# Retention branch projection: eight sums over one half of the features, then the other, and two expert weights' places in SBUF

## What is computed

```python
y_a = o_gla.astype(u.dtype) @ w_br_gla                  # (256, 1024) @ (1024, 1024)
y_b = o_ret.astype(u.dtype) @ w_br_ret                  # (256, 2048) @ (2048, 1024)
merged = (jax.nn.sigmoid(mga.astype(jnp.float32)) * y_a.astype(jnp.float32)
          + jax.nn.sigmoid(mgb.astype(jnp.float32)) * y_b.astype(jnp.float32))
return merged.astype(u.dtype) @ w_out                   # (256, 1024) @ (1024, 1024)
...
def run_block(args):                                    # experts: all 32, 6 MB of weights each
    e, tok, w = args
    xb = t[tok]
    hid = jax.nn.silu(xb @ wg[e]) * (xb @ wu[e])
    return ((hid @ wd[e]).astype(jnp.float32) * w[:, None])
```

## Time and profile before

| | |
|---|---|
| median of 3 executions | 1547.41 us (1546.74, 1547.41, 1552.07) |
| the profiled execution's own time | 1544.61 us |
| its span in the trace | 1543.3 us |
| PE busy / DVE / ACT over the span | 91% / 56% / 44% |
| granted TensorE clock, mean | 0.972 |
| dense work of block 1, retention branch within it | 0 to 428 us, 357 to 403 us |
| router | 428 to 441 us |
| experts | 441 to 875 us |
| block 2 | 875 to 1543 us |

### The profile page before, as it was taken

How to read it: one execution, slowest core, us unless ns; L and a number is a source line. 1 busy time by engine, 2 the same in 40 slices (tenths; PEclk the granted TensorE clock), 3 DMA queues, 4 the chain that set the end, 5 groups by cost and what they waited for, 6 DMA issues and landing times.

```text
span 1543.3 us, 27434 instructions
## 1 busy us (share of the span) xinstructions
PE 1405.4 (91%) x11609; PEld 1190.4 (77%) x11609; DVE 865.6 (56%) x1558; ACT 682.1 (44%) x1185; POOL 10.6 (1%) x10
## 2 busy tenths in 40 slices
PE   7999999999989867777777699999999999899998
PEld 7999899899966434443443389999999986699997
DVE  6776463475522211211121378988888768688776
ACT  6544454553442111111111366565555467565553
POOL 1000000000000000000000010000000000000000
PEclk9999999999989998999999999999999999999999
DMA  7455354469799999999999744236555333446551
GB/s 239 145 159 162 110 167 135 164 209 336 285 409 424 426 425 422 426 426 425 425 426 426 299 157 140 95 114 209 194 184 190 127 124 104 142 153 203 191 180 66
DMA packets 170641, 372.05 MB, mean 241 GB/s; under 512 B 6912, under 2 KB 137088, under 8 KB 145936
## 3 DMA queue, kind: packets, MB, share of 16 engines
q1 hardware_dynamic: 170512, 370.22, 64.4%
HBM read 369.15 MB, written 1.05 MB: 240 GB/s over the span
## 4 chain that ended last, share of the span: by engine, by line
PE 63%; DMA 22%; DVE 8%; ACT 5%; issue 2%; SPq 1%; DVEq 0%; ACTq 0%
PE bank L602 16%; PE bank L604 16%; PE bank L603 16%; DMA wu<-in_expert_w_up_dram 16%; PE bank L1724 4%; DMA wu<-in_expert_w_down_dram 3%; DVE lo L566 3%; ACT hi L555 2%; PE bank L833 2%; PE bank L1696 2%; PE bank L1762 1%; PE bank L1776 1%; DMA raw<-in_w_in_dram 1%; PE bank L942 1%; PE bank L967 1%
## 5 line engine op out<-in xcount | busy, mean ns | idle before, releaser
L566 DVE TENSOR_TENSOR lo<-raw,hi 128x1024 fp32r<-128x1024 f32 (+2 forms) x315 | 376.4, 1217 | 176.7 <-ACT hi L555 175.9
L602 PE MATMUL bank<-XH,hi 128*128 128x256 f32 x1416 | 405.7, 286 | 5.8 <-DVE lo L566 2.7
L603 PE MATMUL bank<-XL,hi 128*128 128x256 f32 x1416 | 400.7, 283 | 0.0
L604 PE MATMUL bank<-XH,lo 128*128 128x256 f32 x1416 | 400.7, 283 | 0.0
L555 ACT ACTIVATE hi<-raw 128x1024 fp32r<-128x1024 f32 (+2 forms) x315 | 321.4, 1049 | 117.8 <-PE bank L604 70.8
L602 PEld LDWEIGHTS bank<-XH,hi 128*128 128x128 f32 x1416 | 271.4, 192 | 14.0 <-issue 10.6
L603 PEld LDWEIGHTS bank<-XL,hi 128*128 128x128 f32 x1416 | 271.4, 192 | 0.8
L604 PEld LDWEIGHTS bank<-XH,lo 128*128 128x128 f32 x1416 | 271.3, 192 | 0.0
L1724 PE MATMUL bank<-wu,xg 128*32 128x256 f32 x2048 | 168.5, 429 | 57.0 <-DMA wu<-in_expert_w_up_dram 51.6
L1724 PEld LDWEIGHTS bank<-wu,xg 128*32 128x32 f32 x2048 | 72.0, 120 | 129.2 <-DMA wu<-in_expert_w_up_dram 69.5
L1762 PE MATMUL bank<-wu,hidT 128*32 128x256 f32 x1024 | 73.8, 402 | 35.6 <-DMA wu<-in_expert_w_down_dram 25.1
(11 more groups left out here) (383 smaller groups left out, 2173.4 us busy)
## 6 DMA issues: line engine op xcount, KB each, us to landing
wu<-in_expert_w_gate_dram SPq DMA_DIRECT2D x64, 1024.0 KB, 26.7
wu<-in_expert_w_up_dram SPq DMA_DIRECT2D x64, 1024.0 KB, 26.5
wu<-in_expert_w_down_dram SPq DMA_DIRECT2D x64, 1024.0 KB, 26.8
raw<-in_w_in_dram SPq DMA_DIRECT2D x44, 1024.0 KB, 5.2
raw<-in_ffn_w_up_dram SPq DMA_DIRECT2D x44, 1024.0 KB, 5.0
raw<-in_ffn_w_down_dram SPq DMA_DIRECT2D x22, 1024.0 KB, 5.0
raw<-in_hgrn_w_in_dram SPq DMA_DIRECT2D x16, 1024.0 KB, 5.4
raw<-in_w_branch_ret_dram SPq DMA_DIRECT2D x8, 1024.0 KB, 6.7
```

The costliest lines, as they stand in the source:

```text
L566: dve.tensor_tensor(lo_of(u), v, hi_of(u), ALU.subtract).then_inc(*WL.inc(u))
L602: pe.matmul(dst, first[0], first[1], start=start, stop=False)
L603: pe.matmul(dst, second[0], second[1], start=False, stop=False)
L604: return pe.matmul(dst, third[0], third[1], start=False, stop=stop)
```

## The change

All eight sums are now open at once, in eight PSUM banks. PE goes through the first half of the features for sums 0 to 7 (units 97 to 104), then through the second half for sums 0 to 7 (units 105 to 112). The weight tiles are taken in that order. A sum is therefore finished at each of the last eight units, where before two were finished at the end of each four. `act_split` and `dve_split` run one unit further ahead of the steps of a sum: eight splits stand alone (for units 97 + i), and in the loop over the sums the split of unit 108 + i comes before the steps of sum i.

Places 8 and 9 of the expert weights are now two that are free once the first half of the features is done (`us_at + 8192 * 5` and `gla_at`, where the first half of `RH` and `RL` lie). Their loads wait for unit 104 in place of unit 112 and are issued after tile 55 in place of after tile 59. Load 10 now stands ahead of tile 60, in their old place.

```diff
-    for i in range(4):
-        for h in range(2):
+    for h in range(2):
+        for i in range(4):
             add(cols(D, w_re[D * h:D * h + D, :], 256 * i), halves_c)
...
-    where += [us_at + 8192 * i for i in (5, 6, 7)] + [gla_at, gla_at + 8192] + [us_at + 8192 * i for i in (0, 1)]
+    where += [us_at + 8192 * 5, gla_at] + [us_at + 8192 * i for i in (6, 7)] + [gla_at + 8192] + [us_at + 8192 * i for i in (0, 1)]
...
         def re_unit(t, i):
 
-            return 2 * (t - i % 2) + 1 + i % 2
+            return 2 * t + 7 + i
+
+        def re_bank(t, i):
+
+            return (t + i) % 4 if i < 4 else i
...
+            sp.wait_ge(*WU.got(2 * 52))
+            sp_weights(8)
+            sp_weights(9)
             while at_tile[0] < TILES1 - 1:
                 sp_tile()
             sp.wait_ge(*WU.got(2 * 56))
-            sp_weights(8)
-            sp_weights(9)
+            sp_weights(10)
             sp_tile()
-            for n in range(10, 13):
+            for n in (11, 12):
                 sp_weights(n)
...
-            for i in range(0, 8, 2):
-                bs = bank[t % 4], bank[(t + 1) % 4]
...
+            for h in range(2):
+                for i in range(8):
+                    b, u = bank[re_bank(t, i)], 2 * t - 1 + 8 * h + i
+                    for s, key in b.taken if h == 0 else []:
                         pe.wait_ge(*s.got(*key))
...
+                    b.taken = [(MIX.dve, ("re", i))]
+            t += 8
...
             for i in range(8):
-                act_split(re_unit(t, i) + 3)
+                act_split(2 * t - 1 + i + 4)
+            for i in range(8):
+                act_split(re_unit(t, i) + 4)
                 act.wait_ge(*MIX.dve.got("merged", i))
...
             for i in range(8):
-                dve_split(re_unit(t, i) + 3)
+                dve_split(2 * t - 1 + i + 4)
+            for i in range(8):
+                dve_split(re_unit(t, i) + 4)
                 dve.wait_ge(*WU.got(re_unit(t, i)))
                 dve.wait_ge(*MIX.act.got("mb", i // 2))
-                dve.tensor_tensor(sig_b[:, i, :], b_[t % 4][:, 0:T], sig_b[:, i, :], ALU.mult).then_inc(*MIX.dve.inc("re", i))
+                dve.tensor_tensor(sig_b[:, i, :], b_[re_bank(t, i)][:, 0:T], sig_b[:, i, :], ALU.mult).then_inc(*MIX.dve.inc("re", i))
```

More of the change, by code:

```diff
@@ L1330, in pe_mixer @@
                 t += 1
-            for i in range(0, 8, 2):
-                bs = bank[t % 4], bank[(t + 1) % 4]
-                for b in bs:
-                    for s, key in b.taken:
+            for h in range(2):
+                for i in range(8):
+                    b, u = bank[re_bank(t, i)], 2 * t - 1 + 8 * h + i
+                    for s, key in b.taken if h == 0 else []:
                         pe.wait_ge(*s.got(*key))
[L1336 to L1349, removed]
+                    pe.wait_ge(*WH.got(u))
+                    pe.wait_ge(*WL.got(u))
+                    for k in range(8):
+                        kk = 8 * h + k
+                        pe.wait_ge(*RET.act.got("RH", kk // 4))
+                        pe.wait_ge(*RET.dve.got("RL", kk // 4))
+                        done = three(b.ap[:, 0:T], hi_of(u)[:, k, :], lo_of(u)[:, k, :], RH[:, kk, :], RL[:, kk, :],
+                                     False, kk == 0, kk == 15)
+                    done.then_inc(*WU.inc(u))
+                    b.taken = [(MIX.dve, ("re", i))]
+            t += 8
             merged = lambda k: [(MIX.act, ("OH", k)), (MIX.dve, ("OL", k))]
@@ L1419, in act_mixer @@
                 act.activation(OH[:, i, :], sig_a[:, i, :], ACT.Copy).then_inc(*MIX.act.inc("OH", i))
-                t += 1
+            t += 8
             for i in range(4):
```

## The result

The changed kernel takes 1556.71 us (median of 17, 1548.72 to 1561.08), the kernel before 1546.91 (median of 17). The ratio is 1.0056, 95% interval 1.0045 to 1.0067: slower by 8.7 us (the medians alone differ by 9.8), a little over the 0.5% that was named as the bound. The forecast was 1552.2 us, slower by 4.8, with a range up to 1557.0, so the result lies only just inside it. The direction, the place and the mechanism came out; the size was nearly double. Two terms were too small: the clock, and what DMA loses behind load 22.

The account below looks back on a forecast made before the run. PE bounds the retention branch, DMA the experts. Stall 4.4 plus clock 1.7 make PE 6.1 us late; less 3.2 of queued work, plus 1.4 restart and 0.5 refill: +4.8, 1552.2 us, range 1545.5 to 1557.0.

Parts of the forecast that it names:

- Nothing to win on PE: Retention branch: PE is already busy throughout with the same 384 matmuls, so the new order of sums costs or wins 0.
- The bunched steps: Border to `o1`: eight rounds of 3.46 us exceed PE's 2.85 us unit, so PE resumes 4.4 us late.
- tile 56 would hold the ring: Sums' chain of waits: tile 56, queued behind loads 8 and 9, lands late and delays the rounds by 1.0 us.
- splits one unit ahead keep PE fed for free: Retention sums: low parts ready at least 1.4 us before PE needs them, 0.4 with the late tile; no cost.
- The clock, +1.7: `o1` after the stall: one stretch of 3.41 us at half clock costs half its length, 1.7 us.
- the refill, +0.5: Experts behind load 22: loads 24 and 25 wait on PE until the queue is deep again, 0.5 us.
- The sign that DMA would be full from load 22 on: Expert stream in the trace after: DMA at full rate from load 22, issued at about 450 us.
- The early loads: Loads 8 and 9: 4.9 us of transfer moved out buy nothing beyond 3.2 us; the queue runs dry before load 22.
- (A): Border to `o1`: same stall without low clock, PE 4.4 us late, total 1550.5 us; chance 0.25.
- (B): `o1` and router: three low stretches cost 5.1 us, router up to 1 more, stream 8.7 us late, 1556.1 us; chance 0.11.
- (C): Steps of the sums: rounds stay under 2.85 us, PE wins 0.4 us, stream 2.2 us earlier, 1545.2 us; chance 0.11.
- (D): Expert stream: both early loads count in full, 4.9 us, plus PE's 0.4, giving 1542.1 us; chance 0.03.

Follow-up runs that it names:

- the ring cut: Changed kernel with DVE's split of unit 108 + i moved behind the product and addition of sum i: 1544.11 us, ratio 0.9983.
- the second trace: Trace of the changed kernel measured once more, nothing altered: 1555.87 us, ratio 1.0048 to the kernel before.
- the last pair of kernels: Changed kernel with the DVE split moved later and 32 unread matmuls in the router's gap, loads 8 and 9 early or late: 0.9966 and 0.9979.
- Filling the stall: Changed kernel plus 27 unread matmuls on PE before its waits for sums 6 and 7 in `o1`: ratio 1.0019.
- the kernel before with the stall of 3.6 us: Kernel before, with DVE forming the router's weights eight times before `OL` of sum 7: ratio 1.0034.
- the fillings: Changed kernel with unread matmuls at the `o1` stall (27), in the router's gap (32), or both: ratios 1.0019, 1.0027, 1.0004.
- With the loads back: Changed kernel with loads 8 and 9 and their places returned to where they were, after tile 59: ratio 1.0049.
- ring cut, loads back: Changed kernel with the DVE split moved later and loads 8 and 9 back after tile 59: ratio 0.9986.
- A gap of 1.64 us: Kernel before, with DVE forming the router's weights four times before `OL` of sum 7: ratio 1.0004.

## Why the prediction came out as it did

**Nothing to win on PE: right.** The retention branch is full in both traces (46.30 of 46.30).

**The bunched steps: right, with one slip.** From the last gated step, unit 112 was to end at 45.6 and PE to go on at 52.8 (410.0 - 357.16). It went on at 53.2 (408.89 - 355.70). That is 4.8 us later than before (405.58 - 357.16 = 48.4) where 4.4 was forecast, a little above the bound. Rounds of 3.46 us were forecast and 3.45 to 3.56 measured where no tile was late, 3.95 and 4.22 where tiles 55 and 56 were. That tile 56 would hold the ring was right, tile 55 wasn't seen. The slip is the claim that splits one unit ahead keep PE fed for free: the first gap, 0.98 us, is PE waiting for the low part of unit 114 (`lo` ends at 403.53, PE goes on at 403.63). `o1` takes its second unit after four k-steps, not after eight, and the slack was counted as if each unit lasted 2.85 us. It cost nothing, since `OL` of sums 6 and 7 came later still; the ring cut shows this bunching and nothing else made the slowdown (0.9983).

**The clock, +1.7, and the refill, +0.5: these terms were too small.** Two stretches at half clock followed in place of one. They began inside the gap, at 406.80, where PE went on at 408.89: PE was busy for 4.74 of these 6.83 us, so `o1` itself lost 2.4 us (3.0 in the second trace, busy for 6.01). Load 22 came 7.3 and 7.6 us late where 6.1 was forecast. The larger miss lies behind it. There the sum took off 3.2 us for the work left in the queue and added 1.4 for the restart and 0.5 (bounds 0 and 1.8) for loads 24 and 25, -1.3 in all. DMA was 8.3 and 11.6 us behind, so the two traces have +1.0 and +4.0 at this step. Where the router's low stretch went on into the first experts, DMA starved a second time, since at half clock PE gives places back more slowly than DMA fills them; the two traces of the ring cut, 10.2 and 30.7 us of low clock with load 22 at the same point, show it: DMA is 7.3 us further behind in the second. Between them stand only the two loads, worth 1.5 us in the same measure in the last pair of kernels, and the stretch at 54 us, which the first has and the second has not. Filling the stall brought 4.5 to 5.7 us back in the total where 1.7 was forecast. The sign that DMA would be full from load 22 on failed too. In the changed kernel's trace the stretch from load 22 to 505 us runs below the rate of the earlier trace rows:

```profile
450.00:505.00 55.00, 54.30 (x714) 35.74 (x718) 13.02 (x32) 15.13 (x50) 0.00 (x0) 0.99 0.97 396
```

(396 GB/s, and 370 from 450 to 505 us in the second trace, against 413; a part of this is the restart of the dry queue.) In the kernel before with the stall of 3.6 us, whose router was slow for 30.7 us, it is plainer, here beside the kernel before:

```profile
456.00:468.00 12.00, 12.00 (x91) 6.97 (x94) 1.01 (x4) 3.52 (x10) 0.00 (x0) 0.50 0.48 181
```

```profile
456.00:468.00 12.00, 12.00 (x178) 8.16 (x174) 2.83 (x7) 3.85 (x14) 0.00 (x0) 1.00 1.01 412
```

181 GB/s over 12 us against 412 is 6.5 us of transfer missing (231 x 12 / 425), with PE busy all the time and doing half the matmuls. What settles how long the router stays slow is open: 30.7 us turn up with a stall and without one. Each kernel has one trace or two, and the totals scatter by 3.5 to 12 us within a kernel, so a trace alone doesn't tell whether a stall lengthens it. That the delay raises the mean of the total by more than its length is shown by the changed kernel (4.8 us late at `o1`, 7.0 to 10.4 in the total) and by the fillings, which leave the wait in place and take the total down to 1.0004.

The Trainium skill, in TensorE: Matmul & The Clock Gate, section on HAM oscillation, prices a kernel that waits between matmuls at half of its time at the low clock. By that, the 6.8 us cost 3.4. Here PE was idle for part of them and lost 2.4 to 3.0, and filling the gap was worth 4.5 to 5.7 in the total, likely because loads wait for PE's products.

**The early loads: right that they buy nothing here.** The queue ran dry between load 21 (landed at 436.81 + 9.9 = 446.7) and load 22, as drawn: 6 GB/s from 446 to 450 us. It was short of work earlier too, 154 GB/s from 428 to 432, since load 17 waits for a unit of the late `o1`. The signs had this dip (429 to 433), but the sum's 442.5 for the dry queue left it out. With the loads back the ratio is 1.0049, with them early 1.0048 and 1.0056: no gain and no loss that can be told.

**The rivals.** (A), the same stall at full clock, was put at 1550.5 us, 3.1 over; the kernel that realises it (stall filled) is 0.0019 or 2.9 us over (interval 1.1 to 4.6). PE went on 5.2 us late there and not 4.4, so the terms without the clock at `o1` are near in sum, which does not say that each is right. (B) came nearest to the result in size, 8.7 us for 8.7, and its sign, a second low stretch in `o1`, was there. But it had one stretch more at `o1` than there was, too little at the router, and left out the 0.5 for the refill; that the two numbers are equal is luck. It had a chance of 0.11; with gaps of 2 to 4 us followed by anything from none to three such stretches in the earlier trace rows, that chance was too low. (C) and (D) needed what the ring cut shows: once the round is below PE's unit, the change does win, 2.6 us (C had 2.2 less than before).

## What to carry to other kernels

When work that came in pairs with rests is put in one row, compare the length of one round through all engines, not any engine's busy time, with the time the slowest engine gives it; a ring of waits between two engines that are both half idle can be the bound, and moving a few independent instructions behind the step that others wait for cuts it. Before crediting transfers that are moved out of a DMA-bound stretch, find the first load that waits for compute and see whether the queue is empty when it comes. A stall on TensorE ahead of a DMA-bound stretch can cost more than its length: the half clock that goes with it, and what DMA loses while the slow TensorE gives buffers back.

## What the runs showed of the hardware

A gap of 1.64 us on TensorE before `o1` was followed by no stretch at granted clock 0.50; gaps of 2.9 to 3.6 us in four kernels (five traces) each went with 6.8 us of it, which began inside the gap.

The length of a gap alone does not decide. All fourteen traces have the same wait of PE at 51 us, 2.2 to 2.6 us long, whose code no kernel here changes. Eight of them have 3.4 us at 0.50 behind it and six have none, and the lengths of the two groups overlap (2.23 us with, 2.43 without). What tells them apart is not tested here. It matters for the rest: all five traces with an unfilled stall are among the six without, and those with the stall filled or of 1.64 us are among the eight. So these single traces differ in more than the gap, and that filling pays rests on the totals of 11 and 12 executions each. The router's low stretch, where not filled, was 10.2 us long in three traces of the eight and 13.7 in one; in five traces of the six it was 13.7 to 30.7, in one of these (ring cut, loads back) with no stall at all.

Matmuls that nobody reads paid although they are work on the busiest engine: with 32 of them in the router's 3.9 us gap five kernels were 1.1 to 4.5 us faster by their ratios; of these differences only those of the kernel before and of the changed kernel are clear of the noise.
